# Attention B in another order: pair steps shifted on four engines, scalings on POOL, the bound in the bias row

## What is computed

```python
def swa_mixer(h, w_in, b_in, sinks, w_out, b_out, rel_bias):
    ...
    q, k, v = _split(h @ w_in + b_in, B_SIZES)      # 16 query heads, 2 key/value heads of 64
    ...
    logits = jnp.einsum('bnqkgd,bnskd->bnkgqs', q, kk).astype(jnp.float32) * (Dh ** -0.5)
    ...
    logits = logits + jnp.transpose(bias, (2, 3, 0, 1)).astype(jnp.float32)
    logits = jnp.where(mask[None, :, None, None], logits, -jnp.inf)
    sink = jnp.broadcast_to(sinks.reshape(KV, G)[None, None, :, :, None, None].astype(jnp.float32),
                            logits.shape[:-1] + (1,))
    p = jax.nn.softmax(jnp.concatenate([logits, sink], axis=-1), axis=-1)[..., :-1]
    o = jnp.einsum('bnkgqs,bnskd->bnqkgd', p.astype(vv.dtype), vv)
    return o.reshape(B, T, N_HEADS * Dh) @ w_out + b_out
```

## Time and profile before

| | us |
|---|---|
| median of 3 runs | 1210.18 (1208.48 to 1210.74) |
| the profiled execution, its own time | 1209.77 |
| its span | 1208.0 |

### The profile page before, as it was taken

How to read it: one execution, slowest core, us unless ns; L and a number is a source line. 1 busy time by engine, 2 the same in 40 slices (tenths; PEclk the granted TensorE clock), 3 DMA queues, 4 the chain that set the end, 5 groups by cost and what they waited for, 6 DMA issues and landing times.

```text
span 1208.0 us, 16227 instructions
## 1 busy us (share of the span) xinstructions
PE 1165.8 (97%) x5600; PEld 965.4 (80%) x5600; DVE 587.2 (49%) x1031; ACT 463.0 (38%) x857; POOL 580.4 (48%) x319
## 2 busy tenths in 40 slices
PE   7999999999999999999999979799999999999996
PEld 6767889888888888888888768688888888888885
DVE  5479867645544344432221588845543444421111
ACT  5353267754323322332222566633333222322332
POOL 4426658864355444544443653233554445534441
PEclk9999999999999999999999989899999999999998
DMA  8432311123333333223333442113323332233331
GB/s 234 154 126 70 123 34 47 45 71 105 105 88 85 104 104 101 78 67 96 95 95 96 120 105 54 36 36 105 95 80 103 104 104 80 83 89 91 86 94 70
DMA packets 179220, 110.42 MB, mean 91 GB/s; under 512 B 7292, under 2 KB 173367, under 8 KB 179176
## 3 DMA queue, kind: packets, MB, share of 16 engines
q1 hardware_dynamic: 178448, 108.69, 31.5%
q10 hardware_dynamic: 728, 1.17, 0.3%
HBM read 107.70 MB, written 6.33 MB: 94 GB/s over the span
## 4 chain that ended last, share of the span: by engine, by line
PE 84%; DVE 7%; issue 3%; ACT 1%; DMA 1%; POOL 0%; DVEq 0%; ACTq 0%; SPq 0%
PE ps L566 27%; PE ps L568 27%; PE ps L567 27%; PE ps L781 1%; DVE b_prob L1705 1%; PE ps L575 1%; DVE work L1463 1%; DVE b_prob L1684 1%; PE ps L760 1%; DVE work L1447 1%; DVE bpt_lo L1350 1%; DMA raw<-in_b_w_in 1%; PE ps L908 0%; DVE b_rsum L1696 0%; DVE xs_lo L1350 0%
## 5 line engine op out<-in xcount | busy, mean ns | idle before, releaser
L456 POOL TENSOR_TENSOR w_lo<-raw,w_hi 128x1024 fp32r<-128x1024 f32 (+1 forms) x200 | 462.1, 2332 | 509.0 <-ACT w_hi L1002 500.4
L566 PE MATMUL ps<-xs_hi,w_hi 128*128 128x512 f32 (+3 forms) x1024 | 398.9, 390 | 5.4 <-POOL w_lo L456 2.2
L568 PE MATMUL ps<-xs_hi,w_lo 128*128 128x512 f32 (+3 forms) x1024 | 395.2, 386 | 0.0
L567 PE MATMUL ps<-xs_lo,w_hi 128*128 128x512 f32 (+3 forms) x1024 | 395.0, 386 | 0.0
L1002 ACT CAST w_hi<-raw 128x1024 fp32r<-128x1024 f32 (+1 forms) x196 | 179.1, 962 | 433.6 <-PE ps L568 420.8
L566 PEld LDWEIGHTS ps<-xs_hi,w_hi 128*128 128x128 f32 x1024 | 192.7, 188 | 51.1 <-issue 3.4
L567 PEld LDWEIGHTS ps<-xs_lo,w_hi 128*128 128x128 f32 x1024 | 192.7, 188 | 39.2 <-issue 1.1
L568 PEld LDWEIGHTS ps<-xs_hi,w_lo 128*128 128x128 f32 x1024 | 192.6, 188 | 38.7
L566 PE MATMUL ps<-act_hi,w_hi 128*128 128x512 f32 x352 | 139.2, 396 | 0.0
L568 PE MATMUL ps<-act_hi,w_lo 128*128 128x512 f32 x352 | 138.0, 392 | 0.0
L567 PE MATMUL ps<-act_lo,w_hi 128*128 128x512 f32 x352 | 136.6, 388 | 0.0
(11 more groups left out here) (186 smaller groups left out, 1382.0 us busy)
## 6 DMA issues: line engine op xcount, KB each, us to landing
raw<-in_ffn_w_gate_up SPq DMA_DIRECT2D x88, 512.0 KB, 4.9
raw<-in_ffn_w_down SPq DMA_DIRECT2D x32, 384.0 KB, 3.6
raw<-in_a_w_in SPq DMA_DIRECT2D x20, 512.0 KB, 5.1
raw<-in_ffn_w_down SPq DMA_DIRECT2D x32, 320.0 KB, 4.0
raw<-in_b_w_in SPq DMA_DIRECT2D x10, 512.0 KB, 5.2
bias_toep<-bias_row SPq DMA_DIRECT2D x4, 1024.0 KB
toep<-bias_toep SPq DMA_DIRECT2D x16, 256.0 KB, 2.6
raw<-in_a_w_out SPq DMA_DIRECT2D x8, 512.0 KB, 4.1
```

Of the source, the lines that this page charges most:

```text
L456: nc.gpsimd.tensor_tensor(pieces(w_lo, n)[half], pieces(raw, n)[half], pieces(w_hi, n)[half].bitcast(F32), ALU.subtract)\
L566: nc.tensor.matmul(dst, wh, xh, start=start, stop=False, **kw)
L567: nc.tensor.matmul(dst, wh, xl, start=False, stop=False, **kw)
L568: return nc.tensor.matmul(dst, wl, xh, start=False, stop=stop, **kw)
```

## The change

It reorders the steps of a pair on PE, DVE, ACT and POOL, and moves some work between them.

- PE: step k is logits(k), turn(k-2, 0), half of projection k+2, weighing(k-3), turn(k-2, 1), the other half. Projection 2 stands behind logits(0), not ahead. In steps 6 and 7 and behind them, slices of tiles 0 to 3 of the output projection fill in (`b_out`), in an order written out by hand; `out_rest` starts at tile 4. The banks of the tiles are new (`B_OUT_BANK`).
- `bpt_hi` and `bpt_lo` hold two pairs.
- All 64 scalings go from DVE to POOL (`b_normalise`). `bq_lo` goes from POOL to DVE (`b_q_part`), which adds the bias in the same instruction; ACT adds it in the copy to `bq_hi`, and `b_bias` is gone. POOL's additions into `b_bm` are gone: the bound of the window is in a second bias row of 384 distances, so the row is 1024 long, and one more DMA of 2 MB spreads it. The copies of the sinks are gone.
- `b_invert` takes both halves of a pair in one sum and one reciprocal; POOL's scaling waits for it.

```diff
@@ tables()
+    place = np.concatenate([np.arange(ROW_A), np.arange(ROW_A - ROW_B, ROW_A)])
...
-    t[BUCKETS, C_HOT:] = np.where(np.arange(GLEN) >= T, BIG, 0)
+    t[BUCKETS, C_HOT:] = np.where((place >= T) | (np.arange(GLEN) >= ROW_A) & (place < T - P), BIG, 0)
@@ SP, between the a_w_out slabs and the first FFN
+            sp.wait_ge(neg_done, 4 * H)
+            skew_b = bass.AP(tensor=bias_row.tensor, offset=ROW_A + P - 1, ap=[[GLEN, H], [-1, P], [1, 2 * P]])
+            sp.dma_start(bias_toep[:, :, 0:2 * P], skew_b).then_inc(toep_out, 16)
@@ POOL
-            for j in range(DM):
...
-                nc.gpsimd.tensor_tensor(bq_lo[:, par, :], bq_raw[:, par, :],
...
-                    nc.gpsimd.tensor_tensor(b_bm[:, par, a, :], b_toep[:, par, a, :], window, ALU.add)\
+            def b_normalise(k, a):
+
+                pool.wait_ge(brinv_done, k + 1)
+                for i in range(NB):
+                    n = P if i == 0 else 2 * P
+                    at = b_prob[:, k % 2, a, OFFB[i]:OFFB[i] + n]
+                    nc.gpsimd.tensor_scalar(at, at, b_rinv[:, k % 2, a, i:i + 1], None, ALU.mult)\
+                        .then_inc(bnrm_done[a], 1)
+
+            split_lo(S_BQ + 2)
+            for k in range(DM):
                 for a in range(2):
+                    b_normalise(k, a)
+                if k in (1, 3, 5):
+                    split_lo(S_BQ + 3 + k // 2)
@@ PE
-            for k in range(DM + 2):
-                b_step(k)
+            for k in range(DM):
+                b_logits(k)
+                if k >= 2:
+                    b_turn(k - 2, 0, k)
+                if k < DM - 2:
+                    b_project(k + 2, range(0, DM // 2))
+                else:
+                    b_out(0, range(k - 6, k - 5))
+                if k >= 3:
+                    b_weigh(k - 3)
+                if k >= 2:
+                    b_turn(k - 2, 1, k)
+                if k < DM - 2:
+                    b_project(k + 2, range(DM // 2, DM))
+            b_out(1, range(0, 2))
+            b_turn(DM - 2, 0, DM)
+            b_out(0, range(2, 3))
+            b_weigh(DM - 3)
+            b_turn(DM - 2, 1, DM)
...
+            out_rest(S_BO, 3, bo_hi, bo_lo, 4)
@@ ACT
-            b_bias(0)
             b_q(0)
-            b_bias(1)
+            split_after(S_BQ)
             b_q(1)
...
+            for k in range(DM):
+                if k in (2, 4, 6):
+                    split_after(S_BQ + k // 2)
+                if k >= 2:
+                    b_turned_hi(k - 2, 0)
+                if 1 <= k < DM - 1:
+                    b_q(k + 1)
+                b_exponents(k, 0)
+                if k >= 2:
+                    b_turned_hi(k - 2, 1)
+                if k >= 3:
+                    b_heads_hi(k - 3)
+                b_exponents(k, 1)
@@ DVE
+            def b_q_part(j):
+
+                dve.wait_ge(bqh_done, j + 1)
+                nc.vector.scalar_tensor_tensor(bq_lo[:, j % 2, :], bq_raw[:, j % 2, :], nq_bias[:, j:j + 1],
+                                               bq_hi[:, j % 2, :].bitcast(F32), ALU.add, ALU.subtract)\
+                    .then_inc(bql_done, 1)
+
             b_scale(0)
             b_scale(1)
+            b_q_part(0)
+            b_q_part(1)
...
+            for k in range(DM):
+                if 1 <= k < DM - 1:
+                    b_scale(k + 1)
+                if k >= 1:
+                    b_invert(k - 1)
+                b_lowest(k, 0)
+                if k >= 2:
+                    b_turned_lo(k - 2, 0)
+                if 1 <= k < DM - 1:
+                    b_q_part(k + 1)
+                b_lowest(k, 1)
+                if k >= 2:
+                    b_turned_lo(k - 2, 1)
+                if k >= 3:
+                    b_heads_lo(k - 3)
```

More of the change, by code:

```diff
@@ L36 @@
 WIN = 7 * P
[L38 to L39 removed]
+C_ID, C_DUP, C_CAUSAL, C_HOT = 0, P, 2 * P, 3 * P
+ROW_A, ROW_B = 640, 384
+GLEN = ROW_A + ROW_B
 C_END = C_HOT + GLEN
@@ new lines, in b_out @@
+            def b_out(m, ks):
+                n = S_BO + m // 2
+                for k in ks:
+                    pe.wait_ge(bol_done, k + 1)
+                    if k == 0:
+                        pe.wait_ge(lo_done, 2 * n + 2)
+                        pe.wait_ge(*((bqr_done, DM) if m == 0 else (bneg_done, 8 * DM)))
+                    c = k * 256 + (m % 2) * P
+                    last = mm3(ps[:, B_OUT_BANK[m], :], w_hi[:, n % 2, c:c + P], w_lo[:, n % 2, c:c + P],
+                               bo_hi[:, k, :], bo_lo[:, k, :], k == 0, k == DM - 1)
+                    if k == DM - 1:
+                        last.then_inc(unit_done, 1)
@@ L977, in _ @@
+            for m in range(3):
+                b_out(m, range(5, 6))
+            for m in range(2):
+                b_out(m, range(6, 7))
+            b_out(3, range(2, 3))
+            for m in range(2):
+                b_out(m, range(7, 8))
+            b_out(2, range(6, 8))
+            b_out(3, range(3, 8))
+            out_rest(S_BO, 3, bo_hi, bo_lo, 4)
             feed_forward(1, 3, S_F1, S_D1)
@@ new lines, in b_exponents @@
+            def b_exponents(k, a):
+                par, j = k % 2, k + a * (H // 2)
+                for i in range(NB):
+                    n = P if i == 0 else 2 * P
+                    at = b_prob[:, par, a, OFFB[i]:OFFB[i] + n]
+                    act.wait_ge(bneg_done, 8 * k + 4 * a + i + 1)
+                    nc.scalar.activation(at, at, ACT.Exp, bias=b_low[:, par, a, i:i + 1], scale=-1.0,
+                                         accum_out=b_rsum[:, par, a, i:i + 1])
+                nc.scalar.activation(b_sinkp[:, par, a, :], b_low[:, par, a, :], ACT.Exp,
+                                     bias=sink[:, j:j + 1]).then_inc(bsinkp_done, 1)
@@ L1569, in out_proj, with out_proj_b @@
                         new_x(e, m, v % 2, GAIN[e])
+            def out_proj_b(u0, e, bias):
+                for m in range(DM):
+                    dve.wait_ge(unit_done, u0 + 1 + m)
+                    nc.vector.scalar_tensor_tensor(x[:, m, :], ps[:, B_OUT_BANK[m], :], params[:, bias + m:bias + m + 1],
+                                                   x[:, m, :], ALU.add, ALU.add).then_inc(x_new, 1)
+                    new_x(e, m, m % 2, GAIN[e])
             def feed_forward(layer, e, u_gu, u_d):
@@ L1716, in _ @@
+            b_invert(DM - 1)
+            for h in (DM - 2, DM - 1):
+                b_turned_lo(h, 0)
+                b_turned_lo(h, 1)
+                b_heads_lo(h - 1)
+            b_heads_lo(DM - 1)
+            out_proj_b(U_BO, 3, B_OUT)
             feed_forward(1, 3, U_F1, U_D1)
```

300 lines of the change are left out of this document (116 added, 184 removed).

## The result

The changed kernel takes 1197.83 us (1195.45 to 1199.46, 4 runs), the kernel before 1209.52 beside it (4 runs): ratio 0.991, 95% interval 0.9898 to 0.9922. That is 11.7 us, and the forecast was 11.2. Two later comparisons gave 0.9905 (0.9885 to 0.9924) and 0.9899 (0.9884 to 0.9913). The total is right; several of the terms in it are off, by about 5 us to either side, and cancel.

A forecast was written before the change was run, and what follows sets the result against it. PE was taken as full outside attention B and held up there by DVE; 19.6 − 1.3 − 1.1 − 2.7 − 2.1 − 1.2 = 11.2 us off 1209.77 gave 1198.6, stated as 1199.0 us, range 1194 to 1205.

The forecast's parts named there:

- At stake, 19.6 us: Attention B: 15.9 us of PE idle plus 3.7 us lost to half clock, all that an edit there could give back.
- rival B: Attention B's tail: waits bring another clock drop, 2 us, and POOL is 3 us late for turns; 1204 us, chance 0.16.
- Part 1: PE's step in attention B: no work goes, some 13 more changes of kind at 0.1 us each; cost 1.3 us.
- Part 2: All scaling to POOL in attention B: 6.75 us a pair, POOL keeps up, 3 us or more ahead of turns; cost 0.
- rival D: Attention B: POOL becomes the bound from 1.10 us a scaling block, making the kernel slower; chance 0.06.
- Part 3: DVE in attention B: 8.3 to 10.5 us of work per 11.6 us step; the big waits and both clock drops go.
- Part 5: Steps 6 and 7 of attention B: waits cost 2.7 us, and `b_invert(6)` stalled behind POOL's slab costs 2.1 us.
- Part 6: Table row of 1024 instead of 640: L638 multiplies 512 columns, not 128, ahead of full PE; cost 1.2 us.
- Part 7: Extra 2 MB DMA ahead of the first FFN slab: covered at 254 GB/s, cost 0; at half the rate, 4 to 8 us.
- Part 8: Output projection: four tiles finish in the loop's tail instead of two, the DVE and ACT backlog clears by tile 7; cost 0.
- Rival A: Attention B: the `b_invert(6)` stall misses, the turned order costs nothing, only 1.6 us of tail remains; 1194.5 us, chance 0.12.
- rival C: Worse attention B tail, plus the 2 MB transfer delaying the first FFN slab 4 us more: nothing measurable, 1208 us, chance 0.05.

## Why the prediction came out right

The total was right by luck: errors of 5 us on either side cancel. The mechanism in attention B, which carries the gain, was right.

- **At stake, 19.6 us: right in kind.** All of the long waits and both drops behind them went. The idle fell from 15.9 to 4.1 us, as forecast for the three that stay: 1.1 before the first logits (1.1), 1.1 before logits(7) (1.0), 1.9 before `b_out(1)` (1.6). One drop of 3.4 us came at 764.6, which the forecast did not have (it named a stretch at 0.50 as a sign against it); it is 1.7 us. It came behind the waits of 1.1 and 1.9 us, as rival B had it.
- **Part 1, +1.3 us: wrong in sign.** By starts of matmuls, with work at half clock counted half, PE's time by kind is, before and after: projections 33.6 and 34.3, logits 12.9 and 12.8, turns 13.0 and 11.9, weighings 23.0 and 22.0, output projection 44.5 and 44.6. The cut projection costs 0.7; turns and weighings are 2.1 cheaper, and that they no longer stand at the edge of a wait is a likely reason, not a shown one. The net is about 1.5 us less, not 1.3 more. I priced each change of kind from first rows against 0.28 us, which I called an inner matmul; in the earlier trace rows it is the first of the weighing, so the rows never showed that price.
- **Part 2, POOL: right**, 6.6 to 6.9 us a pair against 6.75. The margin was larger than the 3 us of my walk, and rival D's threshold rested on that: the kernel lost its whole gain at 54.7 + 25.2 = 79.9 us for 64 blocks, 1.25 us each, where the prediction's sum has (54 + 11.2 + 3) / 64 = 1.07.
- **Part 3, DVE: right for the steps** (11.5 us, forecast 11.6 to 11.8), but the reason was only half told. The prediction had both DVE's load and POOL's slabs; the two runs with scalings on DVE show that the slabs are nearly all of it. The stretched scalings of the earlier trace rows were the cause and not a sign. The four there took 2.15, 2.46, 1.35 and 0.81 us, each until 0.1 to 0.15 us behind one POOL instruction, and only two of those were slab work. The third was `bq_lo`, the fourth `b_bm`, which the change takes off POOL as well. Timelines of DVE and of POOL in the kernel before:

```profile
709.40 1.35 DVE L1705 TENSOR_SCALAR b_prob<-b_prob,b_rinv 128x256 f32<-128x256 f32 x1
```

```profile
709.30 1.30 POOL L545 TENSOR_TENSOR bq_lo<-bq_raw,bq_hi 128x512 fp32r<-128x512 f32 x1
```

- **Part 5, the stall: +2.1 was not spent.** It is 0.75 us on DVE and nothing on PE here. It is real, as the 1.97 us of the run with a heavier POOL show, but it depends on 1 us of phase (0.45 us into the slab instruction there, 1.5 here). A term of that sort belongs in the range, not whole in the sum.
- **Part 6, the row: right**, 1.0 us by the trace of the run without it, against 1.2. In the two profiles PE was 2.9 us behind at 30 us and 1.4 at 125; how much of that is the row's stands in the last section.
- **Part 7, the 2 MB DMA: wrong, 0 against about 3 us.** This is the step that failed. I took 254 GB/s from a stretch that is mostly loads from DRAM to SBUF for a copy from DRAM to DRAM with a step back in each row. It ran at 114 to 131 GB/s. The text had the bound, "at half the rate, 4 to 8 us", and I took the wrong end, although a row of the same kind stood in the table that the earlier trace rows is from. From 44 to 48 us the kernel before moves nothing but its own spread of `bias_toep`, at 102 GB/s:

```profile
44.00:48.00 4.00, 4.00 (x19) 3.34 (x18) 0.05 (x1) 1.41 (x2) 4.00 (x2) 1.00 0.26 102
```

Of the 5.2 us by which the slab is late, 3.1 reached PE in this profile, and 2.3 to 5.8 in the ten with the transfer in this place.

- **Part 8: right**, no wait in the output projection.

In the two profiles: 12.4 + 2.8 (part 1) + 2.1 (part 5) − 1.7 (clock) − 0.3 (tail) = 15.3 us, and 15.4 were measured in attention B; 1.4 and 3.1 ahead of it are the 4.5. Rival A's mechanism held in part: no stall on PE and no cost of order, but logits(7) did wait 1.1 us, which A had left out. The place that rival C names took about 3 us back. Rivals D and E fall: neither POOL nor ACT is waited for in attention B.

Left open: why the drops at 764 and at about 300 come in some executions and not in others. A kernel with `b_q_part(0)` ahead of `b_scale(1)`, which should shorten the first wait, was not run.

## What to carry to other kernels

When DVE seems overloaded, look first whether its long instructions coincide with POOL's. Then shortening or moving POOL's work may be worth more than relieving DVE, and moving the pieces that clash onto POOL itself puts an end to most of the clash (DVE's sums still stand) even at 2.7 times the price for each. A reordering, a second buffer and a move to another engine can be worth 15 us together and less than nothing where one of them is missing, so don't judge such a change by its parts. And price a DMA by a transfer of the same kind, look at which load is next in that queue, and issue what isn't urgent early (here it was in pieces too).

## What the runs showed of the hardware

- A copy from DRAM to DRAM, 2 MB in rows of 1 KB, ran with all 16 DMA engines busy at 114 to 131 GB/s, and the load queued behind it came 5.2 us late. In 8 pieces, earlier, it was not to be seen. The spread of the kernel before, in rows of 2 KB, moved 102 GB/s at a DMA share of 0.26; why the shares differ is open.
- A scaling on DVE that met a POOL instruction with two inputs in SBUF ended 0.15 us behind it: 0.59 us beside one of 0.46, 2.53 beside one of 2.41, 1.35 beside one of 1.30. A sum of 8 elements with both inputs in SBUF stood for 1.8 us. DVE's minima, which read a bank and `b_toep`, kept their 0.48 us beside the same slab (at 759.0 in the run with one more scaling).
- The clock at the start differs from execution to execution of one kernel. In two profiled executions of the changed kernel it was granted at full speed from 12.4 and from 20.2 us on, and the second row matmul took, timelines of PE,

```profile
13.05 1.02 PE L642 MATMUL ps<-hot,rel_sb 33*16 33x512 f32 x2
```

in the one and

```profile
13.50 1.91 PE L642 MATMUL ps<-hot,rel_sb 33*16 33x512 f32 x2
```

in the other. By 30 us they are 3.1 us apart. The early one had a drop to half clock of 3.4 us at 111.4, which took back 1.6 of it, and the late one had none. So the 2.9 us that the changed kernel seemed to lose at its start against the kernel before are mostly of this sort, and not of the row: one profile each would have charged the row with three times its price.
- With the same work and the same waits in attention B, three executions had the drop at 764 and took 131.9 us, and two (the transfer spread out, the row by copies) had none and took 130.3.
